# Strassen sets of a float32 MLP: weight blocks in fixed slots, low parts of the moving sums in reading order, and one weight sum made on VectorE instead of by an adding transfer

## The chip, the cores and the metric

The kernel runs on one core of a Trainium2 chip. Its metric is the device time of one execution in microseconds (us). The core has a matrix engine (TensorE, PE), VectorE (DVE), ScalarE (ACT), GpSimd (POOL) and SyncE (SP), which each take their instructions in order and meet at semaphores. SP and POOL start transfers here.

## The reference, cut to what matters

One layer of a streaming encoder in float32, for 512 prompt frames, 16 meta tokens and 64 sample frames. What the change touches is the MLP, on 576 tokens, with `D_MODEL` 1024 and `D_FF` 4096:

```python
h = _layer_norm(ALPHA * h + (mix @ w_out + b_out), ln1_g, ln1_b)
f = jnp.square(jax.nn.relu(h @ w_mlp1 + b_mlp1)) @ w_mlp2 + b_mlp2
h = _layer_norm(ALPHA * h + f, ln2_g, ln2_b)
```

## The kernel before

**Splitting.** A float32 product is made of three matmuls on a faster type: each operand is rounded to a high part (`hi`) and the difference to a low part (`lo`); hi x hi, hi x lo and lo x hi are added in PSUM. Of a weight block ACT makes the high part (`op_hi`, L1839) and DVE the low part (`op_lo`, L2695). Of a moving operand of the second MLP product it is ACT's `v_hi` (L1895) or `block_hi` (L1881) and DVE's `set_lo` (L2764).

**Sets.** The first 8 output blocks of the first MLP product are done plainly. All the rest but the last quarter of the second product is done in 12 sets (`SETS`), t = 0 to 11, each a 2 x 2 block product in Winograd's form with 7 instead of 8 block products: "out" (second product) for t = 0, 1, 4, 5, 8, 9 and "in" (first product) for t = 2, 3, 6, 7, 10, 11. The 7 steps of a set are s = 0 to 6. A step is 24 matmuls of 288 columns with 128 x 128 weights (`block_product`, L1268 to L1270).

**Weight blocks.** A set has 4 blocks of 128 x 1024 in DRAM (`wsets_d[t, 0..3]`, 512 KB each). The 7 stationary operands are, in the order of the steps: AL = block 0; SI = 2 + 3; X = 0 + 2 + 3; DE = 1; AP = 0 + 2; DP = 1 + X; GA = block 3. There are five slots: `raw` 0 to 3 and `w_fifth` (slot 4). `set_slots(t)` gives a (AL, then X), b (DE, then DP), c (SI), d (AP) and g (GA); a/c and b/d change places from set to set. SP loads block 2 into c and POOL adds block 3 with an adding transfer (L3203); SP loads block 2 into d and POOL adds block 0 (L3205). X and DP are made on DVE (`x_sum` L2681 in step 6 of the set before, `dp_sum` L2687 in step 2).

**Order around it.** Everything is written out by hand. High and low parts have three homes in turn; in step s of set t ACT makes the high and DVE the low part of the operand for step s + 2, and ACT may do so once step s - 1 is done. PE's step waits for its low part (`s_lo`), for its PSUM banks and for its moving operand. The banks: step 2 waits for `first_copied` (ACT, L1845), step 4 for `third_sum` (DVE, L2725; in an "out" set for its second `out_add`, L2713), step 6 for `fourth_sum` (DVE, L2733; or the fourth `out_add`).

**The moving sums.** An "in" set gives four blocks of relu-squared, C11, C22, C12, C21 (ACT: L1874 relu, L1881 high part, L1886 square in place). From them DVE makes V5, T3, V6, V4 (`v_sum`, L2744 to L2754). With B11, B22 and B21 (C11, C22, C21) they are the seven moving operands of the next "out" sets, read in the order B11, V5, V6, B21, T3, B22, V4. Much of this is done under the next set, as its tail (`set_tail` on ACT, `tail` and `sums` on DVE). An "out" set with group 0 (t = 4, 8) follows at once on the "in" set that makes its operands and waits for each in turn (`moving_ready`); C11 of a set is rounded in step 4, C22 in 5, C12 in 6, C21 in step 0 of the next. Sets with a tail under them are t = 3, 4, 7, 8 and 11. In sets 0 and 1 ACT and DVE have extra work: `residual2` (L1906), `hs_round`, `hs_low`.

Of the kernel before, what the change touches and what calls it, by code (L numbers as in the profile page):

```python
# [69 lines left out]

def set_slots(t):


    return (1, 3, 0, 2, 4) if t % 2 == 0 else (0, 2, 1, 3, 4)


def source_slot(t, s):
    a, b, c, d, g = set_slots(t)
    return (a, c, a, b, d, b, g)[s]
# [125 lines left out]
def encoder_step(nc, x, wstream, wsets_d, vecs_d, bv_d, kc_d, vc_d, state_d, wpool_d, y_out, k_out, v_out, s_out):  # L205
    with ExitStack() as ctx:
# [185 lines left out]
        al_in, de_in, ga_in, si_base = x_in[0]  # L392
        ap_base = x_in[1][0]
        si_in, ap_in = sem("si_in"), sem("ap_in")
        x_made, dp_made = sem("x_made"), sem("dp_made")
# [262 lines left out]
        def _(sp):  # L658
# [30 lines left out]
            sp.wait_ge(lo_split, U_MLP1 + HIDDEN - 3)  # L689
            load_block(0, set_slots(0)[2], 2, si_base)  # L690
            sp.wait_ge(lo_split, U_MLP1 + HIDDEN - 2)
            load_block(0, set_slots(0)[0], 0, al_in)
            sp.wait_ge(lo_split, U_MLP1 + HIDDEN - 1)
            load_block(0, set_slots(0)[3], 2, ap_base)
            sp.wait_ge(lo_split, U_MLP1 + HIDDEN)
            load_block(0, set_slots(0)[1], 1, de_in)
            sp.wait_ge(f_lo_done, F_TILES)
            load_block(0, set_slots(0)[4], 3, ga_in)
            for t in range(1, N_SETS):
                a, b, c, d, g = set_slots(t)  # L700
                o = OPS * (t - 1)
                sp.wait_ge(s_lo, o + W_SI + 1)
                sp.wait_ge(x_made, t)
                load_block(t, a, 0, al_in)
                sp.wait_ge(s_lo, o + W_X + 1)
                sp.wait_ge(dp_made, t)
                load_block(t, c, 2, si_base)
                sp.wait_ge(s_lo, o + W_AP + 1)
                load_block(t, b, 1, de_in)
                sp.wait_ge(s_lo, o + W_DP + 1)  # L710
                load_block(t, d, 2, ap_base)
                sp.wait_ge(s_lo, o + W_GA + 1)
                load_block(t, g, 3, ga_in)
# [637 lines left out]
        def _(act):  # L1351
# [472 lines left out]
            def op_hi(o):  # L1824
                t, s = divmod(o, OPS)
                if o >= OPS * N_SETS:
                    return
                landed = {W_AL: al_in, W_SI: si_in, W_DE: de_in, W_AP: ap_in, W_GA: ga_in}.get(s)
                if landed is not None:
                    act.wait_ge(landed, (0 if s in (W_SI, W_AP) else SET_IN) + 16 * (t + 1))  # L1830
                elif s == W_X:
                    act.wait_ge(x_made, t + 1)
                else:
                    act.wait_ge(dp_made, t + 1)
                if o < 3:
                    act.wait_ge(unit_done, U_MLP1 + HIDDEN - 2 + o)
                else:
                    act.wait_ge(op_done, o - 2)
                nc.scalar.activation(op_home(o)[0], set_home(source_slot(t, s)), ACT.Copy).then_inc(s_hi, 1)  # L1839

# [107 lines left out]
            def set_tail(t, s):  # L1948

                _, p, g = SETS[t]  # L1950
                if s == 0:
                    block_relu(t, C21)
                    if p == 3:
                        block_hi(t, C21)
                    block_plain(t, C21)
                elif p < 3:
                    v_hi(t, T3)
                    v_hi(t, V4)

            for t in range(N_SETS):  # L1960
# [3 lines left out]
                for s in range(OPS):  # L1964
                    if s == 0 and tail is not None:
                        set_tail(tail, 0)
                        op_hi(o + 2)
                        if SETS[tail][1] < 3:
                            v_hi(tail, V6)
                            v_hi(tail, B21)  # L1970
                        continue
# [10 lines left out]
                    if kind == "in" and s == 6:  # L1982
                        block_relu(t, C12)
                        if p == 3:
                            block_hi(t, C12)
                        block_plain(t, C12)
                    op_hi(o + s + 2)
                    if t == 0 and s == 0:
                        for f in (V6, T3, V4):
                            sum_hi(f, PRS - 1)  # L1990
                    if s == 1 and tail is not None:
                        set_tail(tail, 1)
                    if kind == "in" and s == 5:
                        block_relu(t, C22)
                        block_hi(t, C22)
                        block_plain(t, C22)
                    if kind == "in" and s == 6 and p < 3:
                        v_hi(t, V5)
                    if t == 0 and s < 4:
                        residual2((4, 0, 2, 6)[s])  # L2000
                        residual2((5, 1, 3, 7)[s])
                    if t == 1 and 1 <= s <= 4:
# [88 lines left out]
        def _(dve):  # L2091
# [583 lines left out]
            def x_sum(t):  # L2675

                if t == N_SETS:
                    return
                a, _, c, _, _ = set_slots(t)
                dve.wait_ge(si_in, 16 * (t + 1))  # L2680
                tt(set_home(a), set_home(c), set_home(a), ALU.add).then_inc(x_made, 1)  # L2681

            def dp_sum(t):

                a, b, _, _, _ = set_slots(t)
                dve.wait_ge(x_made, t + 1)
                tt(set_home(b), set_home(b), set_home(a), ALU.add).then_inc(dp_made, 1)  # L2687

            def op_lo(o):
# [133 lines left out]
            for t in range(N_SETS):  # L2823
# [162 lines left out]
        def _(pool):  # L2986
# [213 lines left out]
            for t in range(N_SETS):  # L3200
                _, _, c, d, _ = set_slots(t)
# [98 lines left out]
```

## Time and profile before

| | us |
|---|---|
| median of 3 runs | 799.43 |
| lowest, highest | 797.58, 800.34 |
| the profiled execution | 798.34 |
| its span | 796.6 |

The profile is of one execution. Its page gives the busy time of each engine; matmul rows overlap, so a busy PE isn't yet a PE without gaps, and the gaps are read in the timeline. A row of the timeline names in square brackets how long its engine sat idle before it and whose event ended that. A wait for several events is put down to the one that came last by the profile. L numbers are lines of the kernel before.

### The profile page before, as it was taken

To read this page: it belongs to the slowest core of one execution; us is meant where nothing else is said; L and a number is where in the kernel's file an instruction comes from. 1 tells how busy PE (TensorE), PEld (TensorE's weight loads), DVE (VectorE), ACT (ScalarE), POOL (GpSimd) and SP (SyncE) were. 2 spreads that over 40 slices of the span, in tenths; PEclk is the share of its full clock that TensorE was granted. 3 is DMA by queue.
4 is the path that set the end of the run, shared out by engine and by line. 5 is a ranking of instruction groups with operands and counts; after the bars stand their busy time and mean duration, and the time that the engine had idled before them with its cause. 6 is when DMAs were issued, how large, how long until landed. Compare 5 with 4: busy or idle time off the path is not lost.

```text
span 796.6 us, 14048 instructions
## 1 busy us (share of the span) xinstructions
PE 776.4 (97%) x5720; PEld 748.6 (94%) x5720; DVE 519.6 (65%) x762; ACT 426.8 (54%) x666; POOL 145.9 (18%) x195
## 2 busy tenths in 40 slices
PE   8999999999999999999999999999999999999995
PEld 7999899999989999999999999998999999999994
DVE  6823344754546476876968979687775887655644
ACT  5633345655646465563655556587336763477324
POOL 2100000472220110006640000000000000000356
PEclk9999999999999999999999999999999999999998
DMA  8632131112111112233112366645666456653203
GB/s 313 261 123 95 58 114 53 54 57 81 53 53 54 53 53 73 88 114 125 58 50 80 80 190 176 163 123 143 186 173 171 130 141 175 173 125 133 80 2 119
DMA packets 27070, 90.57 MB, mean 114 GB/s; under 512 B 2864, under 2 KB 7104, under 8 KB 26624
## 3 DMA queue, kind: packets, MB, share of 16 engines
q1 hardware_dynamic: 22592, 74.26, 27.3%
q0 software_dynamic: 4000, 15.10, 10.3%
q8 instruction: 45, 0.74, 0.4%
q10 hardware_dynamic: 416, 0.33, 0.1%
q14 instruction: 17, 0.14, 0.1%
HBM read 84.84 MB, written 4.85 MB: 113 GB/s over the span
## 4 chain that ended last, share of the span: by engine, by line
PE 80%; DVE 7%; ACT 6%; issue 3%; DMA 3%; DVEq 0%; ACTq 0%; POOL 0%; SPq 0%; POOLq 0%
PE lin L751 8%; PE lin L752 8%; PE lin L753 8%; PE z L1268 6%; PE z L1269 6%; PE z L1270 6%; PE z L1007 3%; DMA raw<-w_sets 3%; PE lin L1145 3%; PE lin L1146 3%; PE lin L1147 3%; PE lin L1285 2%; PE lin L1287 2%; PE lin L1286 2%; PE lin L1268 2%
## 5 line engine op out<-in xcount | busy, mean ns | idle before, releaser
L751 PE MATMUL lin<-h_hi,whi 128*128 128x288 f32 (+1 forms) x448 | 133.8, 299 | 0.0
L752 PE MATMUL lin<-h_lo,whi 128*128 128x288 f32 (+1 forms) x448 | 132.5, 296 | 0.0
L753 PE MATMUL lin<-h_hi,wlo 128*128 128x288 f32 (+1 forms) x448 | 132.0, 295 | 0.0
L751 PEld LDWEIGHTS lin<-h_hi,whi 128*128 128x128 f32 x448 | 84.2, 188 | 1.3 <-issue 1.1
L752 PEld LDWEIGHTS lin<-h_lo,whi 128*128 128x128 f32 x448 | 84.2, 188 | 0.1
L753 PEld LDWEIGHTS lin<-h_hi,wlo 128*128 128x128 f32 x448 | 84.3, 188 | 0.0
L1839 ACT ACTIVATE whi<-raw 128x1024 fp32r<-128x1024 f32 x48 | 50.7, 1056 | 55.4 <-DMA raw<-w_sets 18.0
L2695 DVE TENSOR_TENSOR wlo<-raw,whi 128x1024 fp32r<-128x1024 f32 x48 | 58.7, 1223 | 22.3 <-ACT whi L1839 22.3
L2098 DVE TENSOR_TENSOR wlo<-raw,whi 128x1024 fp32r<-128x1024 f32 x41 | 50.9, 1242 | 28.6 <-ACT whi L1361 26.5
L1361 ACT ACTIVATE whi<-raw 128x1024 fp32r<-128x1024 f32 x38 | 40.0, 1053 | 50.5 <-PE lin L753 32.5
L1268 PE MATMUL z<-f_ops,whi 128*128 128x288 f32 x176 | 52.8, 300 | 3.4 <-DVE f_ops L2764 2.0
L1269 PE MATMUL z<-f_ops,whi 128*128 128x288 f32 x176 | 52.3, 297 | 0.0
L1270 PE MATMUL z<-f_ops,wlo 128*128 128x288 f32 x176 | 52.2, 296 | 0.0
L3203 POOL DMA_DIRECT2D raw<-w_sets x12 | 10.5, 872 | 191.9 <-DMA raw<-w_sets 191.9
L1839 ACT ACTIVATE third_hi<-raw 128x1024 fp32r<-128x1024 f32 x24 | 25.3, 1056 | 25.8 <-DVE raw L2681 7.3
L1268 PEld LDWEIGHTS z<-f_ops,whi 128*128 128x128 f32 x176 | 33.8, 192 | 3.8 <-issue 2.2
L2695 DVE TENSOR_TENSOR third_lo<-raw,third_hi 128x1024 fp32r<-128x1024 f32 x24 | 29.3, 1222 | 11.3 <-ACT third_hi L1839 11.3
L2319 DVE SCALAR_TENSOR_TENSOR sa<-z,sa 128x512 f32<-128x512 f32 (+4 forms) x25 | 19.8, 795 | 25.6 <-ACT sa L1544 25.4
L1270 PEld LDWEIGHTS z<-f_ops,wlo 128*128 128x128 f32 x176 | 33.7, 192 | 0.0
L1269 PEld LDWEIGHTS z<-f_ops,whi 128*128 128x128 f32 x176 | 33.7, 191 | 0.0
L2282 DVE TENSOR_SCALAR gates<-lin,vecs 128x288 f32<-128x288 f32 x16 | 8.2, 516 | 34.6 <-PE lin L753 34.6
L1268 PE MATMUL z<-hs_hi,whi 128*128 128x288 f32 x96 | 28.6, 298 | 0.9 <-DVE z L2725 0.6
(456 smaller groups left out, 2572.7 us busy)
## 6 DMA issues: line engine op xcount, KB each, us to landing
raw<-w_stream SPq DMA_DIRECT2D x64, 512.0 KB, 3.2
raw<-w_sets SPq DMA_DIRECT2D x48, 512.0 KB, 3.6
raw<-w_sets POOLq DMA_DIRECT2D x24, 512.0 KB, 6.9
w_fifth<-w_sets SPq DMA_DIRECT2D x12, 512.0 KB, 6.2
r<-x_t SPq DMA_DIRECT2D x8, 296.0 KB, 4.4
kcache<-k_cache SPq DMA_DIRECT2D x1, 2048.0 KB, 9.8
vcache<-v_cache SPq DMA_DIRECT2D x1, 2048.0 KB, 8.0
y<-r SPq DMA_DIRECT2D x8, 160.0 KB, 1.8
```

The source lines that it names most:

```text
L751: pe.matmul(out, w_h, hi, start=first, stop=False)
L752: pe.matmul(out, w_h, lo, start=False, stop=False)
L753: return pe.matmul(out, w_l, hi, start=False, stop=last)
L1007: last = pe.matmul(zf[:, d:d + w], stationary[:, :], part[:, src + at:src + at + w], start=False, stop=True, skip_group_check=True)
L1145: pe.matmul(out, w_h, hi, start=first, stop=False)
L1268: pe.matmul(out, w_h, hi, start=s < 2 and i == 0, stop=False, skip_group_check=True)
L1269: pe.matmul(out, w_h, lo, start=False, stop=False, skip_group_check=True)
L1270: last = pe.matmul(out, w_l, hi, start=False, stop=i == PRS - 1, skip_group_check=True)
L1361: nc.scalar.activation(whi[:, j % SPLIT, :], raw[:, j, :], ACT.Copy).then_inc(hi_split, 1)
L1839: nc.scalar.activation(op_home(o)[0], set_home(source_slot(t, s)), ACT.Copy).then_inc(s_hi, 1)
L2098: tt(wlo[:, j % SPLIT, :], raw[:, j, :], whi[:, j % SPLIT, :].bitcast(F32), ALU.subtract)\
L2695: tt(home[1], set_home(source_slot(t, s)), home[0].bitcast(F32), ALU.subtract).then_inc(s_lo, 1)
```

## The change

The slots are the same for every set: a = 1, b = 3, c = 0, d = 2, g = 4. AP is no longer loaded and added to: DVE makes it as X - GA (`ap_sum`, in step 1). For set 0 GA's block is loaded into d as well, ahead of the rest, and subtracted there. The second adding transfer of a set goes, and so does the load of its base (in set 0 it becomes that load of block 3).

SP now loads c first, once `x_sum` is made, then a, once `dp_sum` is made, then b and g. `dp_sum` goes from step 2 to step 3, ahead of `op_lo`.

The low part of B11 goes behind `op_lo` of step 5, that of V5 from step 0 of the next set to step 6, ahead of `x_sum`. V4's sum goes behind `op_lo` of step 0. B21 stays in step 1, T3 goes from 1 to 2, B22 from 2 to 4 and V4 from 3 to 4. On ACT the rounding of V5 goes ahead of `op_hi` of step 6, that of B21 from step 0 to 1, that of V4 from 1 to 3, and the `residual2` of set 0 from steps 0 to 3 to steps 1, 2, 4, 5.

```diff
-def set_slots(t):
-    return (1, 3, 0, 2, 4) if t % 2 == 0 else (0, 2, 1, 3, 4)
+def set_slots():
+    return 1, 3, 0, 2, 4
@@ sync: loads of the sets
-            load_block(0, set_slots(0)[3], 2, ap_base)
+            load_block(0, set_slots()[3], 3, ga_first)
...
                 sp.wait_ge(s_lo, o + W_SI + 1)
                 sp.wait_ge(x_made, t)
+                load_block(t, c, 2, si_base)
+                sp.wait_ge(dp_made, t)
                 load_block(t, a, 0, al_in)
-                sp.wait_ge(s_lo, o + W_X + 1)
-                sp.wait_ge(dp_made, t)
-                load_block(t, c, 2, si_base)
-                sp.wait_ge(s_lo, o + W_AP + 1)
+                sp.wait_ge(s_lo, o + W_DP + 1)
                 load_block(t, b, 1, de_in)
-                sp.wait_ge(s_lo, o + W_DP + 1)
-                load_block(t, d, 2, ap_base)
                 sp.wait_ge(s_lo, o + W_GA + 1)
                 load_block(t, g, 3, ga_in)
@@ scalar: op_hi
-                elif s == W_X:
-                    act.wait_ge(x_made, t + 1)
+                elif s in (W_X, W_AP):
+                    act.wait_ge(x_made if s == W_X else ap_made, t + 1)
@@ scalar: set_tail and the loop of the sets
-                    v_hi(t, T3)
-                    v_hi(t, V4)
+                    for o in {1: (B21, T3), 3: (V4,)}.get(s, ()):
+                        v_hi(t, o)
...
                             v_hi(tail, V6)
-                            v_hi(tail, B21)
...
                         block_plain(t, C12)
+                        if p < 3:
+                            v_hi(t, V5)
                     op_hi(o + s + 2)
...
-                    if s == 1 and tail is not None:
-                        set_tail(tail, 1)
+                    if s and tail is not None:
+                        set_tail(tail, s)
...
-                    if kind == "in" and s == 6 and p < 3:
-                        v_hi(t, V5)
-                    if t == 0 and s < 4:
-                        residual2((4, 0, 2, 6)[s])
-                        residual2((5, 1, 3, 7)[s])
+                    if t == 0 and s in (1, 2, 4, 5):
+                        m = {1: 4, 2: 0, 4: 2, 5: 6}[s]
+                        residual2(m)
+                        residual2(m + 1)
@@ vector
+            def ap_sum(t):
+                a, _, _, d, g = set_slots()
+                if t == 0:
+                    g = d
+                    dve.wait_ge(ga_first, SET_IN + 16)
+                else:
+                    dve.wait_ge(ga_in, SET_IN + 16 * (t + 1))
+                dve.wait_ge(x_made, t + 1)
+                tt(set_home(d), set_home(a), set_home(g), ALU.subtract).then_inc(ap_made, 1)
...
-                        if sums:
-                            set_lo(tail, V5)
-                            v_sum(tail, V4)
                     if inner:
                         if s == 3:
                             third_sum(t)
                         elif s == 5:
                             fourth_sum(t)
-                            last_lo(t, C11) if p == 3 else set_lo(t, B11)
+                        elif s == 6 and p < 3:
+                            v_sum(t, V5)
+                            v_sum(t, T3)
                     elif s >= 2:
                         out_add(t, s - 2)
-                    if s == 6 and inner and p < 3:
-                        v_sum(t, V5)
-                        v_sum(t, T3)
-                    if s == 2:
+                    if s == 3:
                         dp_sum(t)
+                    elif s == 1:
+                        ap_sum(t)
                     op_lo(o + s + 2)
...
                     if sums:
-                        for f in {0: (V6,), 1: (B21, T3), 2: (B22,), 3: (V4,)}.get(s, ()):
+                        if s == 0:
+                            v_sum(tail, V4)
+                        for f in {0: (V6,), 1: (B21,), 2: (T3,), 4: (B22, V4)}.get(s, ()):
                             set_lo(tail, f)
...
+                    if inner and s == 5:
+                        last_lo(t, C11) if p == 3 else set_lo(t, B11)
...
                             v_sum(t, V6)
+                            set_lo(t, V5)
                     if s == 6:
                         x_sum(t + 1)
@@ gpsimd
                 pool.dma_start(set_home(c), wsets_d[t, 3], accum_op=ALU.add).then_inc(si_in, 16)
-                pool.wait_ge(ap_base, SET_IN + 16 * (t + 1))
-                pool.dma_start(set_home(d), wsets_d[t, 0], accum_op=ALU.add).then_inc(ap_in, 16)
```

## Rows read from the trace of the kernel before

**Rows 1.** The page: the span, and busy us of PE and DVE.

```profile
span 796.6 us, 14048 instructions
...
PE 776.4 (97%) x5720; PEld 748.6 (94%) x5720; DVE 519.6 (65%) x762; ACT 426.8 (54%) x666; POOL 145.9 (18%) x195
```

**Rows 2.** Windows of sets 6, 7, 8 and 9: length, then busy us.

```profile
core 0: us, PE busy (x) PEld busy (x) DVE busy (x) ACT busy (x) POOL busy (x), PEclk, DMA share, GB/s
593.95:616.28 22.33, 22.33 (x170) 22.33 (x169) 13.09 (x14) 13.69 (x20) 1.73 (x2) 1.00 0.72 173
616.28:639.93 23.65, 22.80 (x170) 22.40 (x169) 20.01 (x24) 18.16 (x29) 1.73 (x2) 1.00 0.51 147
639.93:663.83 23.90, 22.53 (x171) 22.13 (x169) 19.37 (x23) 11.79 (x17) 0.92 (x3) 1.00 0.60 153
663.83:685.86 22.03, 22.03 (x171) 22.03 (x169) 15.44 (x16) 8.81 (x9) 2.55 (x3) 1.00 0.66 170
```

**Rows 3.** Timeline of PE, first matmuls of steps: start us, us, ..., [idle before].

```profile
461.88 0.37 PE L1268 MATMUL z<-f_ops,whi 128*128 128x288 f32 x1 [1.43 <-DVE wlo L2695]
...
550.99 0.37 PE L1268 MATMUL z<-f_ops,whi 128*128 128x288 f32 x1 [1.99 <-DVE f_ops L2764]
...
623.09 0.37 PE L1268 MATMUL lin<-hs_hi,third_hi 128*128 128x288 f32 x1 [0.26 <-ACT z L1845]
...
630.28 0.37 PE L1268 MATMUL lin<-hs_hi,whi 128*128 128x288 f32 x1 [0.59 <-DVE z L2725]
...
636.74 0.30 PE L1268 MATMUL lin<-hs_hi,whi 128*128 128x288 f32 x1
...
644.41 0.37 PE L1268 MATMUL z<-f_ops,third_hi 128*128 128x288 f32 x1 [1.14 <-DVE f_ops L2764]
```

**Rows 4.** Window behind the wait at 550.99; the number before the last two is PEclk.

```profile
551.65:555.05 3.40, 3.40 (x16) 3.40 (x15) 2.76 (x3) 3.40 (x6) 0.00 (x0) 0.50 0.36 135
```

**Rows 5.** Groups by line on DVE: busy us, mean ns of one.

```profile
L2695 DVE TENSOR_TENSOR wlo<-raw,whi 128x1024 fp32r<-128x1024 f32 x48 | 58.7, 1223 | 22.3 <-ACT whi L1839 22.3
...
L2681 DVE TENSOR_TENSOR raw<-raw 128x1024 f32<-128x1024 f32 x12 | 14.6, 1219 | 0.0
...
L2764 DVE TENSOR_TENSOR f_ops<-f_plain,f_ops 128x576 fp32r<-128x576 f32 x24 | 17.7, 752 | 0.0
```

**Rows 6.** Timeline of DVE in sets 6 to 8.

```profile
615.80 0.76 DVE L2744 TENSOR_TENSOR f_plain<-f_b,f_b 128x576 f32<-128x576 f32 x1 [2.02 <-ACT f_b L1886]
...
618.95 1.22 DVE L2681 TENSOR_TENSOR raw<-raw 128x1024 f32<-128x1024 f32 x1
...
629.38 0.76 DVE L2725 TENSOR_TENSOR z<-lin,f_plain 128x576 f32<-128x576 f32 x1
...
642.38 1.22 DVE L2681 TENSOR_TENSOR raw<-raw 128x1024 f32<-128x1024 f32 x1
643.51 0.75 DVE L2764 TENSOR_TENSOR f_ops<-f_plain,f_ops 128x576 fp32r<-128x576 f32 x1
```

**Rows 7.** Timeline of ACT in set 0 and in sets 7 and 8.

```profile
461.15 0.63 ACT L1845 ACTIVATE lin<-z 128x576 f32<-128x576 f32 x1
...
616.62 0.67 ACT L1895 ACTIVATE f_ops<-f_plain 128x576 fp32r<-128x576 f32 x1
...
629.73 0.90 ACT L1874 ACTIVATE f_b<-z,vecs 128x288 f32<-128x288 f32 x2 [0.98 <-PE z L1270]
...
631.83 1.04 ACT L1839 ACTIVATE whi<-w_fifth 128x1024 fp32r<-128x1024 f32 x1
...
639.47 1.06 ACT L1839 ACTIVATE third_hi<-raw 128x1024 fp32r<-128x1024 f32 x1 [0.89 <-DMA raw<-w_sets]
```

**Rows 8.** The adding transfer for SI, L3203, from issue to landing.

```profile
DMA to landing us min/median/max: 5.4/7.7/9.1
```

**Rows 9.** The loads of the sets by SP, L687, from issue to landing.

```profile
DMA to landing us min/median/max: 3.1/4.0/8.8
```

More of the change, by code:

```diff
@@ L68, in sets_before, with source_slot @@
     return sum(k == kind for k, _, _ in SETS[:t])
-def set_slots(t):
-    return (1, 3, 0, 2, 4) if t % 2 == 0 else (0, 2, 1, 3, 4)
-def source_slot(t, s):
-    a, b, c, d, g = set_slots(t)
+def set_slots():
+    return 1, 3, 0, 2, 4
+def source_slot(s):
+    a, b, c, d, g = set_slots()
     return (a, c, a, b, d, b, g)[s]
@@ L392, in encoder_step @@
         al_in, de_in, ga_in, si_base = x_in[0]
-        ap_base = x_in[1][0]
-        si_in, ap_in = sem("si_in"), sem("ap_in")
+        ga_first = x_in[1][0]
+        si_in, ap_made = sem("si_in"), sem("ap_made")
         x_made, dp_made = sem("x_made"), sem("dp_made")
@@ L689, in _ @@
             sp.wait_ge(lo_split, U_MLP1 + HIDDEN - 3)
-            load_block(0, set_slots(0)[2], 2, si_base)
+            load_block(0, set_slots()[2], 2, si_base)
             sp.wait_ge(lo_split, U_MLP1 + HIDDEN - 2)
-            load_block(0, set_slots(0)[0], 0, al_in)
+            load_block(0, set_slots()[0], 0, al_in)
             sp.wait_ge(lo_split, U_MLP1 + HIDDEN - 1)
-            load_block(0, set_slots(0)[3], 2, ap_base)
+            load_block(0, set_slots()[3], 3, ga_first)
             sp.wait_ge(lo_split, U_MLP1 + HIDDEN)
-            load_block(0, set_slots(0)[1], 1, de_in)
+            load_block(0, set_slots()[1], 1, de_in)
             sp.wait_ge(f_lo_done, F_TILES)
-            load_block(0, set_slots(0)[4], 3, ga_in)
+            load_block(0, set_slots()[4], 3, ga_in)
             for t in range(1, N_SETS):
-                a, b, c, d, g = set_slots(t)
+                a, b, c, d, g = set_slots()
                 o = OPS * (t - 1)
@@ L1827, in op_hi @@
                     return
-                landed = {W_AL: al_in, W_SI: si_in, W_DE: de_in, W_AP: ap_in, W_GA: ga_in}.get(s)
+                landed = {W_AL: al_in, W_SI: si_in, W_DE: de_in, W_GA: ga_in}.get(s)
                 if landed is not None:
-                    act.wait_ge(landed, (0 if s in (W_SI, W_AP) else SET_IN) + 16 * (t + 1))
-                elif s == W_X:
-                    act.wait_ge(x_made, t + 1)
+                    act.wait_ge(landed, (0 if s == W_SI else SET_IN) + 16 * (t + 1))
+                elif s in (W_X, W_AP):
+                    act.wait_ge(x_made if s == W_X else ap_made, t + 1)
                 else:
@@ L1838, in op_hi @@
                     act.wait_ge(op_done, o - 2)
-                nc.scalar.activation(op_home(o)[0], set_home(source_slot(t, s)), ACT.Copy).then_inc(s_hi, 1)
+                nc.scalar.activation(op_home(o)[0], set_home(source_slot(s)), ACT.Copy).then_inc(s_hi, 1)
             def first_copy(t):
@@ L2678, in x_sum @@
                     return
-                a, _, c, _, _ = set_slots(t)
+                a, _, c, _, _ = set_slots()
                 dve.wait_ge(si_in, 16 * (t + 1))
                 tt(set_home(a), set_home(c), set_home(a), ALU.add).then_inc(x_made, 1)
+            def ap_sum(t):
[7 more added lines that the diff above has]
+                tt(set_home(d), set_home(a), set_home(g), ALU.subtract).then_inc(ap_made, 1)
             def dp_sum(t):
-                a, b, _, _, _ = set_slots(t)
+                a, b, _, _, _ = set_slots()
                 dve.wait_ge(x_made, t + 1)
@@ L2694, in op_lo @@
                 dve.wait_ge(s_hi, o + 1)
-                tt(home[1], set_home(source_slot(t, s)), home[0].bitcast(F32), ALU.subtract).then_inc(s_lo, 1)
+                tt(home[1], set_home(source_slot(s)), home[0].bitcast(F32), ALU.subtract).then_inc(s_lo, 1)
             def out_add(t, n):
@@ L3200, in _ @@
             for t in range(N_SETS):
-                _, _, c, d, _ = set_slots(t)
+                _, _, c, d, _ = set_slots()
                 pool.wait_ge(si_base, SET_IN + 16 * (t + 1))
                 pool.dma_start(set_home(c), wsets_d[t, 3], accum_op=ALU.add).then_inc(si_in, 16)
-                pool.wait_ge(ap_base, SET_IN + 16 * (t + 1))
-                pool.dma_start(set_home(d), wsets_d[t, 0], accum_op=ALU.add).then_inc(ap_in, 16)
             pool.wait_ge(n2_d0, 2)
```

## The prediction

> **What bounds the kernel now.** I read first the page, for busy shares. TensorE (PE) is busy 776.4 of 796.6 us and VectorE (DVE) 519.6 [rows 1], so what can be won is what PE waits, and what can be lost is anything that makes PE wait more. Then the sets one by one, as windows [rows 2]. Set 9 takes 22.03 us, 3.15 a step, and is the pace of an "out" set without a wait; set 6 takes 22.33, 3.19 a step, the pace of an "in" set. Set 7 takes 23.65 and set 8 23.90. There DVE is busy 20.01 of 23.65 us, against 13.09 in set 6 and 15.44 in set 9. So the moving sums that are finished under the next set load DVE to 85% just where PE waits. Sets 3 and 4 are built the same way. I call 3 and 4, and 7 and 8, a crossing.
>
> Then the timeline of PE, for the waits themselves [rows 3]. Set 7 waits at step 2 (0.26 us shown, step start 623.09 where 616.28 + 2 x 3.19 = 622.66 was due) and at step 4 (0.59, for `third_sum`). Set 8 waits at step 1 (1.14, for V5's low part), set 4 at the same place (1.99), set 0 at step 2 (1.43). Behind the 1.99 the clock was granted at 0.50 for 3.4 us [rows 4]: 1.2 instead of 2.4 GHz. By the windows sets 7 and 8 are 1.3 and 1.9 us over their paces; sets 3 and 4 lose 2.0 more (0.85 of wait, the rest clock), set 0 some 1.6: 10 us in all, and more than that can't be won in the sets.
>
> Last the timelines of DVE and ScalarE (ACT) in the crossing [rows 5, 6, 7]. I write times from the start of set 7, R = 616.28, and hi(n), lo(n) for the rounding on ACT and the difference on DVE of the block for step n (n = 7 and 8 belong to the next set). A long DVE operation lasts 1.22 us, a short one 0.75 [rows 5]; with the next in the queue they follow at 1.14 and 0.67 (642.38 to 643.51 is one long step [rows 6]). A hand-over between ACT and DVE is 0.03 to 0.05, one from PE 0.2.
>
> **Part 1, the transfers.** Gone are the load and the adding transfer for the AP block, 12 adding transfers and 11 loads of 512 KB. No wait of PE ends on a transfer, so they are worth nothing by themselves. What a transfer does hold is ACT: hi(8) in set 7 began at 639.47 after 0.89 us of waiting for one [rows 7], the adding transfer for SI, which takes 5.4 to 9.1 us [rows 8]. Its base is now loaded right behind `x_sum`, some three steps sooner, so that wait goes. But the rounding of V5 now stands ahead of hi(8) on ACT and waits for V5's sum on DVE. Step 6 began at 636.74 [rows 3]; 0.2 for the hand-over, 1.6 for C12's three operations, 0.76 for V5's sum, 0.67 for its rounding [rows 6, 7], and hi(8) comes at about 640.0. Worth: nothing.
>
> The other side: the AL load now waits for `dp_made` in step 3 (before: `x_sum` in step 0), and is wanted by hi(7) in step 5, 4.4 us later. Loads from SP land in 3.1 to 8.8 us, median 4.0 [rows 9]: 0 to 4.4 us late, and I take 0 by the median. A gain is excluded, since the load comes later than before.
>
> **Part 2, the subtraction.** `ap_sum` is as long as `x_sum`, 1.22 us [rows 5], 12 times, 14.6 us of DVE. Between crossings DVE has 6 to 9 us of a set free [rows 2], and the block is due a step later than it is made: nothing. In a crossing it is 1.14 us in a full queue.
>
> **Part 3, the order.** Two edits build round trips that were not there. (a) V5: sum on DVE, rounding on ACT, then hi(8) on ACT, lo(8) on DVE, V6's sum, V5's low part, and only then `x_sum`. (b) `dp_sum` stands right ahead of lo(5) in step 3, and hi(5) needs it: DVE 1.22, ACT 1.05, DVE 1.22 in line, with DVE idle in the middle, and in "in" sets ACT's work on C11 behind it. Without a tail of sums (b) fits: from the start of step 3, 0.95 + 1.2 + 1.05 + 1.25 = 4.45 us, and step 5 is due at 6.3. So sets 2, 5, 6, 9, 10, 11 cost nothing. In set 1 the four `hs_low`, twice the columns of a short operation and so by estimate from [rows 5] 1.4 us each, bring `out_add` 3 to about 0.5 us past step 6: +0.5.
>
> The crossing, worked through in queue order. V5 sum ends at 0.3 (615.80 [rows 6]), its rounding at 1.0 (616.62 was its start before, too [rows 7]), hi(1) at 1.95, lo(1) at 3.2; step 1 starts 3.35. V6's sum 3.9, V5 low 4.55, `x_sum` 5.7 (before: 618.95 + 1.22, so 3.9 [rows 6]). hi(2) 6.8, lo(2) 8.05: **step 2 starts 8.2**, before 6.8 (623.09 [rows 3]). V4's sum and V6 low 9.4, `ap_sum` 10.5, lo(3) 11.65, B21 low 12.3, lo(4) 13.5, T3 low 14.1, `third_sum` 14.8, `dp_sum` 15.95. hi(5) 17.05, lo(5) 18.3; step 5 starts 18.45. ACT: V4's rounding 17.6, C11 19.7 (its four operations took from 629.73 to 631.83 [rows 7]), hi(6) 20.6. lo(6) 21.9, then B22 and V4 low, which are now in step 4, 23.2, `fourth_sum` 23.85. Step 6 waits for that: **it starts 24.0**, before 20.46 (636.74 [rows 3]). Set 7 ends at 27.2 instead of 23.65: +3.5.
>
> Set 8, from its own start. C22 and C12 on ACT follow `fourth_sum` and end 0.45; V5 sum 1.25, rounding 1.95, hi(1) 2.9, lo(1) 4.2, V6 sum 4.85, V5 low 5.5: **step 1 at 5.65**, before 4.48 (644.41 [rows 3]). `x_sum` 6.65, hi(2) 7.75, lo(2) 9.0, V4's sum, V6 low 10.35: **step 2 at 10.5**, since an "out" set reads V6 there. `ap_sum`, lo(3), B21 low, `out_add` 0, lo(4), T3 low, `out_add` 1, `dp_sum` end 17.6; hi(5), lo(5) 19.95, `out_add` 2 20.6, lo(6) 21.8, B22 low 22.45: **step 5 at 22.6**, since it reads B22. Then two steps of 3.15: 28.9 instead of 23.90 [rows 2]: +5.0.
>
> Sets 3 and 4 have the same order. Before they lost 2.0 us more, 0.85 at V5's low part (1.99 against 1.14 [rows 3]) and the rest on the clock; the new schedule replaces both, so it is +6.5 for this pair where it is +8.5 for 7 and 8.
>
> Set 0: step 2 began 461.88 [rows 3]. Its wait is put down to DVE, but a step 2 needs `first_copied` as well, and that copy ran 461.15 to 461.78 [rows 7], behind two `residual2`. These move behind hi(3): about -0.7.
>
> **The clock.** Of the waits in the sets of before only the one of 1.99 us is followed by a fall [rows 3, 4]; at 3.15 us for 24 matmuls 26 fit into its 3.40 us, and 16 were in it; that is 1.3 lost, and by half the clock 1.7 at most: I take 1.4. The new schedule has waits of 1.6 to 2.7 us, five in each crossing. A fall ahead of a longer wait costs nothing; behind step 5 of set 4 or 8 it costs 1.4. I count one of these two: +1.4.
> The Trainium skill, TensorE: Matmul & The Clock Gate, in its section on a second failure mode, says that TensorE idling briefly but often between groups of matmuls swings between the two clocks. The trace agrees once in several waits; by that rule every wait would bring a fall, and the sum would be the heavy case below.
>
> **Sum** against the profiled execution, 798.3 us: -0.7 + 0.5 + 6.5 + 8.5 + 1.4 = +16.2, so 814.5; the median of the runs is 1.1 higher: 815.6, said as 815.5. A measurement of this kernel tells about 0.3%, 2.4 us, from no change.
>
> **Rivals.** *Faster: the late transfer was the cause.* The chain of waits of set 8's step 1 leads through the adding transfer. If the sooner SI base and V5's low part ahead of `x_sum` make that step punctual, sets 4 and 8 get back 2.2 + 1.4 and 1.3 (waits with their hand-over), the waits for `third_sum` 0.8 twice, set 0 0.7: 7.2, so 792.2. It decides at V5's low part, which must end by 3.0 in set 8, that is 642.9. Against it: even with set 7 as it was hi(8) comes at 640.0 (above), and lo(8), V6's sum and V5's low part end at 643.6 (before: 643.51 + 0.75 [rows 6]). Chance 0.07.
> The Trainium skill, DMA: Bandwidth & Descriptors, section on issuing engines, says that the queues of all engines run on the same 16 DMA engines and interleave; by this every removed transfer speeds the rest, which would help this rival. No row here prices it.
> *No change*: what V5 wins, `x_sum` loses, and (b) is absorbed: 799.4, chance 0.05. For it: each edit alone is about 1 us. Against: DVE is at 85% in the crossing, with little to absorb it.
> *Half of it*: only step 2 of sets 3 and 7 (1.4 each) and B22 at step 5 of sets 4 and 8 (0.85 each, the least by the length of lo(5), `out_add`, lo(6) and B22 low after step 3) get later: +4.5, so 804. Chance 0.08.
> *Heavy*: falls of the clock also after step 2 of sets 3 and 7 (0.7 net each) and after both steps 5, or the AL load 1 us late at each crossing: 818 to 825. Chance 0.10, half of it over 822.
> The forecast keeps 0.70.
>
> **Range.** 805 to 822: the forecast with 10 below for a queue that recovers between steps, and up into the heavy case. Left out are "faster" 0.07, "no change" 0.05, half of "half of it" 0.04 and half of "heavy" 0.05: 0.21. Faster 0.07, same 0.05, slower 0.88.
>
> **What would show it.** In the changed profile: windows of sets 3 and 7 near 27 us, of 4 and 8 near 28 to 29, the others at 22.0 to 22.4; PE waiting in set 7 at step 2 for lo(2), at step 6 for `fourth_sum`, in set 8 at step 5 for a sum's low part; DVE idle about 1 us ahead of lo(5), released by ACT; nothing at all waiting for SI. It is wrong if `third_sum` of set 7 ends before 13.9 after the set's start, or if set 7's step 6 starts before 21.

## The result and the profile after

| | us |
|---|---|
| median before (4 runs) | 798.96 |
| median changed (4 runs, 815.59 to 817.89) | 816.62 |
| ratio | 1.0222, 95% interval 1.0198 to 1.0246 |
| span of the profiled execution | 796.6 before, 815.3 changed |

The changed kernel is 17.7 us slower; 815.5 was forecast. The two profiled executions differ by 18.7 us in span. Of these the 12 sets, 276.8 us before and 294.9 after, hold 18.0; another 0.5 had gone before the first set began. In the tables a set's length runs from its first matmul to that of the next (for set 11 to the end of its last matmul), and "step n" is the time from the set's start to the first matmul of step n, read from PE's timeline.

| set | before | forecast | changed |
|---|---|---|---|
| 0 | 23.69 | 23.0 | 23.18 |
| 1 | 22.03 | 22.5 | 22.75 |
| 3 | 23.66 | 27.2 | 27.28 |
| 4 | 26.02 | 28.9 | 30.38 |
| 7 | 23.65 | 27.2 | 28.67 |
| 8 | 23.89 | 28.9 | 28.95 |
| the other six | 133.9 | as before | 133.7 |

The windows of sets 6, 7, 8 and 9 of the changed kernel, which answer to [rows 2] (length, busy us of PE, PEld, DVE, ACT and POOL, then PEclk, DMA share, GB/s):

```profile
602.40:624.73 22.33, 22.33 (x170) 22.33 (x169) 13.34 (x14) 13.18 (x19) 0.86 (x1) 1.00 0.43 119
624.73:653.40 28.67, 24.91 (x170) 23.89 (x169) 21.00 (x25) 18.44 (x29) 0.87 (x1) 0.94 0.34 93
653.40:682.36 28.96, 24.43 (x171) 23.82 (x169) 22.62 (x26) 12.96 (x17) 0.87 (x1) 0.94 0.34 91
682.36:704.39 22.03, 22.03 (x171) 22.03 (x169) 16.25 (x17) 7.97 (x8) 0.87 (x1) 1.00 0.44 120
```

DVE's work in set 7 rose by 1.0 us and the set by 5.0. So it isn't the added work that fills the time. The DMA share fell from 0.51 to 0.34, and no time was won by it.

Where PE waits now, by its timeline (start, us, ..., [idle before <-releaser]; L numbers are lines of the kernel whose trace is shown). These rows answer to [rows 3]:

```profile
461.43 0.40 PE L1265 MATMUL z<-f_ops,whi 128*128 128x288 f32 x1 [0.50 <-DVE wlo L2704]
...
555.56 0.37 PE L1265 MATMUL z<-f_ops,whi 128*128 128x288 f32 x1 [2.25 <-DVE f_ops L2773]
...
572.40 0.37 PE L1265 MATMUL z<-f_ops,third_hi 128*128 128x288 f32 x1 [2.35 <-DVE f_ops L2773]
...
632.82 0.40 PE L1265 MATMUL lin<-hs_hi,third_hi 128*128 128x288 f32 x1 [1.37 <-DVE third_lo L2704]
...
648.74 0.58 PE L1265 MATMUL lin<-hs_hi,whi 128*128 128x288 f32 x1 [2.24 <-DVE f_plain L2742]
...
657.58 0.37 PE L1265 MATMUL z<-f_ops,third_hi 128*128 128x288 f32 x1 [0.84 <-DVE f_ops L2773]
...
662.41 0.37 PE L1265 MATMUL z<-f_ops,whi 128*128 128x288 f32 x1 [1.39 <-DVE f_ops L2773]
...
674.44 0.37 PE L1265 MATMUL z<-f_ops,whi 128*128 128x288 f32 x1 [2.30 <-DVE f_ops L2773]
```

In set 7 PE waits at step 2 for lo(2) (L2704), and at step 6 for `fourth_sum` (L2742). In set 8 it waits at steps 1, 2 and 5, each time for the low part of a sum (L2773). The working of the forecast has all of them. The sign that it gave for being wrong did not come either: `third_sum` of set 7 (the row at 638.76 below) ends 14.8 us after the set's start, as worked out, and not before 13.9.

Why they are late stands in DVE's timeline of set 7, which answers to [rows 6] (times from the set's start are these less 624.73):

```profile
624.25 0.76 DVE L2753 TENSOR_TENSOR f_plain<-f_b,f_b 128x576 f32<-128x576 f32 x1 [2.02 <-ACT f_b L1883]
...
626.71 1.23 DVE L2704 TENSOR_TENSOR wlo<-raw,whi 128x1024 fp32r<-128x1024 f32 x1 [1.03 <-ACT whi L1836]
...
629.19 1.22 DVE L2678 TENSOR_TENSOR raw<-raw 128x1024 f32<-128x1024 f32 x1
631.53 1.23 DVE L2704 TENSOR_TENSOR third_lo<-raw,third_hi 128x1024 fp32r<-128x1024 f32 x1 [1.13 <-ACT third_hi L1836]
...
638.76 0.76 DVE L2734 TENSOR_TENSOR z<-lin,f_plain 128x576 f32<-128x576 f32 x1
639.43 1.22 DVE L2696 TENSOR_TENSOR raw<-raw 128x1024 f32<-128x1024 f32 x1
641.77 1.23 DVE L2704 TENSOR_TENSOR third_lo<-raw,third_hi 128x1024 fp32r<-128x1024 f32 x1 [1.13 <-ACT third_hi L1836]
645.36 1.23 DVE L2704 TENSOR_TENSOR wlo<-w_fifth,whi 128x1024 fp32r<-128x1024 f32 x1 [2.37 <-ACT whi L1836]
646.51 1.42 DVE L2773 TENSOR_TENSOR f_ops<-f_plain,f_ops 128x576 fp32r<-128x576 f32 x2
647.84 0.75 DVE L2742 TENSOR_TENSOR f_plain<-lin,f_plain 128x576 f32<-128x576 f32 x1
```

In set 7 the engine with the longest queue stands idle five times, 7.7 us in all, and each time for ACT; before it was three times, 3.6 us. The wait of 2.02 for C12's blocks at the end of the set is the same in both kernels. The other four make 5.7 us, where the kernel before had 1.6: 1.03 after V5's and T3's sums, 1.13 after `x_sum` (L2678), 1.13 after `dp_sum` (L2696) and 2.37 until ACT has done C11. Then two lows (646.51) still stand ahead of `fourth_sum`, on which PE waits.

The adding transfers did what they were said to. On the page of the changed kernel the adding transfers land sooner (7.7 us median for SI before [rows 8]) and are 12 instead of 24:

```profile
raw<-w_sets SPq DMA_DIRECT2D x37, 512.0 KB, 3.3
raw<-w_sets POOLq DMA_DIRECT2D x12, 512.0 KB, 5.4
```

ACT waited for an adding transfer 8 times before, 24.6 us in all, and now once, 1.4 us, in set 0. But in the crossings it now waits for the AL load ahead of hi(7), 0.72 us in set 4 and 1.76 in set 8:

```profile
673.85 1.06 ACT L1836 ACTIVATE third_hi<-raw 128x1024 fp32r<-128x1024 f32 x1 [1.76 <-DMA raw<-w_sets]
```

DVE has other work until 675.54 and PE doesn't wait for this low part, so the lateness costs nothing.

### The profile page after: what moved, and what is told of

The parts are those of the page before. It is cut to its first block, busy times and chain, and to the rows that moved or that the text cites. A ratio compares the mean times of both kernels' runs of the same rounds, so it can differ in the third digit from the quotient of the medians.

```text
span 815.3 us, 14037 instructions
## 1 busy us (share of the span) xinstructions
PE 784.0 (96%) x5719; PEld 754.0 (92%) x5720; DVE 533.3 (65%) x774; ACT 427.0 (52%) x666; POOL 135.6 (17%) x183
## 4 chain that ended last, share of the span: by engine, by line
PE 72%; DVE 13%; ACT 9%; issue 5%; DVEq 0%; ACTq 0%; POOL 0%; POOLq 0%
PE lin L748 8%; PE lin L749 7%; PE lin L750 7%; PE z L1265 4%; PE z L1266 4%; PE z L1267 4%; PE z L1004 3%; DVE wlo L2704 3%; PE lin L1142 3%; PE lin L1143 2%; PE lin L1144 2%; PE lin L1282 2%; PE lin L1284 2%; PE lin L1283 2%; ACT whi L1836 2%
## 5 line engine op out<-in xcount | busy, mean ns | idle before, releaser
L2704 DVE TENSOR_TENSOR wlo<-raw,whi 128x1024 fp32r<-128x1024 f32 x48 | 58.7, 1222 | 26.9 <-ACT whi L1836 26.9
L1265 PE MATMUL z<-f_ops,whi 128*128 128x288 f32 x176 | 53.8, 306 | 6.4 <-DVE f_ops L2773 5.9
L3215 POOL DMA_DIRECT2D raw<-w_sets x12 | 10.5, 872 | 287.7 <-DMA raw<-w_sets 287.7
L1266 PE MATMUL z<-f_ops,whi 128*128 128x288 f32 x176 | 53.0, 301 | 0.0
L2704 DVE TENSOR_TENSOR third_lo<-raw,third_hi 128x1024 fp32r<-128x1024 f32 x24 | 29.4, 1223 | 17.2 <-ACT third_hi L1836 17.2
```

The costliest lines, as they stand in the source:

```text
L1265: pe.matmul(out, w_h, hi, start=s < 2 and i == 0, stop=False, skip_group_check=True)
L1266: pe.matmul(out, w_h, lo, start=False, stop=False, skip_group_check=True)
L2704: tt(home[1], set_home(source_slot(s)), home[0].bitcast(F32), ALU.subtract).then_inc(s_lo, 1)
```

## The experiments

The theory: the order on DVE and ACT costs the time, by V5's place, by that of `dp_sum` and by the late lows of B22 and V4; the subtraction and the transfers cost nearly nothing. The rivals: the 14.6 us that the subtraction adds to DVE, and the later loads. Each ratio is against runs of the kernel before beside it; times are medians of 4 to 10 runs.

**E1, the slots, loads and subtraction alone.** From the changed kernel, the order of the kernel before put back on both engines:

```diff
+                        if sums:
+                            set_lo(tail, V5)
+                            v_sum(tail, V4)
...
-                    if s == 3:
+                    if s == 2:
                         dp_sum(t)
...
-                        for f in {0: (V6,), 1: (B21,), 2: (T3,), 4: (B22, V4)}.get(s, ()):
+                        for f in {0: (V6,), 1: (B21, T3), 2: (B22,), 3: (V4,)}.get(s, ()):
...
-                            set_lo(t, V5)
```

> Fixed slots, the loads and the subtraction of the changed kernel, but every operation of ScalarE and VectorE in the order of the kernel before (dp_sum in step 2, V5's rounding behind hi(8), its low part in step 0 behind x_sum, B22 low in step 2, V4 low in step 3, residual2 in steps 0 to 3). Theory (the two round trips and the late low parts cost the time, the subtraction nothing): sets 3 and 7 0.45 us longer through ap_sum ahead of third_sum, set 8 0.2 shorter and set 4 2.3 shorter because the SI block no longer comes late, so about 797.5 us. Rival VectorE (the 12 x 1.22 = 14.6 us of the subtraction are what went into the time): about 813 us. Rival transfers (later loads from SP): about 815 us, with ScalarE waiting for transfers.

Measured: 797.49 us, ratio 0.9995 (0.9981 to 1.0008). Sets 3 and 7 take 24.05 and 24.03 (0.4 more), sets 4 and 8 23.69 and 23.65 (2.3 and 0.2 less), all as expected. In the profiled executions the sets are 2.1 us shorter in total; in the runs nothing of that is to be seen (797.49 against 797.43). The before of the profile had a fall of the clock in set 4, at a mean granted clock of 0.994. One such fall (3.4 us at half clock) is 0.002 of a run's mean clock, by my estimate, and of the 13 runs of before beside E1 all but the slowest lie at 0.995 to 0.997, as do the ten of E1. So most of these runs probably had no such fall and less to win; that is read from rounded means and isn't shown by a trace.

```profile
614.47:638.51 24.04, 22.81 (x171) 22.40 (x170) 21.19 (x26) 19.05 (x30) 0.86 (x1) 1.00 0.40 111
638.51:662.16 23.65, 22.53 (x171) 22.13 (x169) 22.09 (x26) 11.78 (x16) 0.86 (x1) 1.00 0.43 112
```

With the subtraction DVE is busy 22.09 of 23.65 us in set 8, and the set is no longer than before. The rivals of 813 and 815 us are out.

**E2, the order alone**, on the kernel before with its slots and all its transfers; both engines in the changed order.

> The kernel before with its slots, its transfers and its two adding transfers a set, no subtraction, but with the order of the changed kernel on ScalarE and VectorE, dp_sum in step 3 included. Theory (order): the crossing keeps both round trips and loses only ap_sum's 1.14 us from the queue, about 1.0 us less in sets 3 and 7 and 1.1 less in sets 4 and 8 than in the changed kernel: about 812.5 us, four falls of the clock as there. Rival VectorE (subtraction): about 802 us. Rival transfers (later loads from SP): about 799 us.

Measured: 815.17 us, ratio 1.0234 (1.0208 to 1.0259). The rivals of 802 and 799 us are out, and the order without the subtraction costs as much as the whole change. The sum is made up otherwise than expected, though. The four sets of the crossings take 110.0 us for 115.3 in the changed kernel, with two falls of the clock instead of four. Sets 1, 5, 6 and 9 take 3.8 us more, which the theory's 812.5 did not have. In sets 3 and 5 ACT waits for the old adding transfer, 1.34 and 7.91 us, and their step 1 begins late; in set 3 at 4.73 instead of 3.28:

```profile
526.34 1.06 ACT L1839 ACTIVATE whi<-raw 128x1024 fp32r<-128x1024 f32 x1 [1.34 <-DMA raw<-w_sets]
...
528.71 0.41 PE L1268 MATMUL z<-hs_hi,whi 128*128 128x288 f32 x1 [1.39 <-DVE wlo L2695]
```

So with the new order the old transfers are late now and then, and with the old order the new ones change nothing that the runs show.

**E3 to E6 and E8, parts undone one at a time** in the changed kernel.

E3, V5's rounding, its low part and V4's sum in their old places:

```diff
                         block_plain(t, C12)
-                        if p < 3:
-                            v_hi(t, V5)
                     op_hi(o + s + 2)
...
+                    if kind == "in" and s == 6 and p < 3:
+                        v_hi(t, V5)
...
+                        if sums:
+                            set_lo(tail, V5)
+                            v_sum(tail, V4)
...
-                            set_lo(t, V5)
```

> The changed kernel with one part undone: V5 is rounded behind hi(8) on ScalarE, its low part and V4's sum stand at the start of step 0 of the next set, behind x_sum and ahead of lo(2). dp_sum stays in step 3, B22 and V4 low in step 4. Theory: worked through in queue order, step 2 of sets 3 and 7 begins 6.5 us after the set's start instead of 8.1, step 6 at 22.2 instead of 24.0, step 5 of sets 4 and 8 at 20.2 instead of 22.4: 4.2 us less in each crossing, about 808 us. If V5's place is the whole cause (rival): 800 us. If it is none of it: 816 us.

E4, `dp_sum` in step 2:

```diff
-                    if s == 3:
+                    if s == 2:
                         dp_sum(t)
```

> The changed kernel with one part undone: dp_sum in step 2, ahead of lo(4), as before; the rest as changed, V5's rounding ahead of hi(8) and B22 and V4 low in step 4 included. Theory: ScalarE reaches hi(6) about 2.3 us sooner, step 6 of sets 3 and 7 begins at 22.5 instead of 24.0, but step 4 1.1 us late for third_sum; set 8's step 5 at 20.5 instead of 22.4: 3.6 us less in each crossing, about 809 us. If dp_sum's place is the whole cause (rival): 800 us. If it is none of it: 816 us.

E5, the lows of T3, B22 and V4 in their old steps, and V4's rounding in step 1:

```diff
-                    for o in {1: (B21, T3), 3: (V4,)}.get(s, ()):
+                    for o in {1: (B21, T3, V4)}.get(s, ()):
...
-                        for f in {0: (V6,), 1: (B21,), 2: (T3,), 4: (B22, V4)}.get(s, ()):
+                        for f in {0: (V6,), 1: (B21, T3), 2: (B22,), 3: (V4,)}.get(s, ()):
```

> The changed kernel with one part undone: T3 low in step 1, B22 low in step 2, V4 low in step 3 and V4's rounding in step 1, as before; both round trips stay. Theory: step 6 of sets 3 and 7 begins at 22.9 instead of 24.0, and step 5 of sets 4 and 8 is punctual, but third_sum comes later: 2.9 us less in each crossing, about 811 us. If the late low parts are the cause (rival): 800 us.

E6, E3 and E4 together:

> The changed kernel with both round trips undone: V5's rounding, its low part and V4's sum as before, and dp_sum in step 2; B22 and V4 low stay in step 4. Theory: in queue order step 6 of sets 3 and 7 is punctual, set 7 takes 23.3 us, set 8 24.9; with set 0's gain about 797 us, within 2 us of the kernel before. If the late low parts of B22 and V4 are a third cause by themselves (rival): above 802 us.

E8, of E3 only the rounding on ACT; V5's low part stays ahead of `x_sum`:

> The changed kernel with half of the V5 part undone: V5 is rounded behind hi(8) again, but its low part stays ahead of x_sum in step 6 and V4's sum behind lo(2). It tells the round trip through ScalarE from the longer queue ahead of x_sum. Theory: step 2 of sets 3 and 7 begins at 7.05 instead of 8.1, step 6 at 22.95, step 5 of sets 4 and 8 at 21.6: 2.1 us less in each crossing, about 812 us, against 805 where x_sum's place is put back as well. If the round trip alone is what V5's move costs (rival): 805 us.

Measured, with step starts of set 7 and 8 from PE's timeline:

| | us | ratio, interval | 7: step 2 | 7: step 6 | set 7 | 8: step 5 | set 8 | falls in the sets |
|---|---|---|---|---|---|---|---|---|
| before | | 1 | 6.81 | 20.46 | 23.65 | 17.60 | 23.89 | 1 |
| changed | 816.62 | 1.0222 | 8.09 | 24.01 | 28.67 | 21.03 | 28.95 | 4 |
| E3 | 804.98 | 1.0098 (1.0081, 1.0115) | 6.41 | 21.66 | 26.45 | 18.56 | 24.93 | 2 |
| E4 | 806.88 | 1.0119 (1.0102, 1.0136) | 8.09 | 22.51 | 25.71 | 20.50 | 26.91 | 0 |
| E5 | 808.18 | 1.0125 (1.0103, 1.0147) | 8.09 | 22.77 | 26.04 | 20.53 | 26.98 | 1 |
| E6 | 798.79 | 1.0004 (0.9989, 1.0019) | 6.41 | 20.18 | 23.37 | 18.40 | 24.82 | 1 |
| E8 | 811.58 | 1.0162 (1.0140, 1.0184) | 6.96 | 22.88 | 27.67 | 19.78 | 27.69 | 4 |

By the ratios, E3 gives back 1.2 points of 2.2, E4 1.0, E5 1.0, and E3 and E4 together (E6) all of it. No single part is the cause, and the one-cause rivals (800 us, in E8 805) and "none of it" (816) are out. E3's and E4's gains add up to that of E6 (2.3 for 2.2). The third part doesn't add: undone alone the late lows are worth 1.0 point, but E6 still has them and is as fast as before. Against E1, which has none of the three (nor the small moves of B21, B11 and `residual2`), it is 0.1 point slower; in the profiles its sets 3 and 7 are 0.7 us shorter each, set 8 is 1.2 longer and set 4, which has a fall of the clock in E6, 2.4. So the late lows cost that much only where the two round trips have used up the room in the queue.

E8 against E3 parts V5's move: with the rounding alone put back step 2 begins at 6.96, which is 1.13 us sooner; `x_sum` behind V5's low part costs the other 0.6.

The expected step starts of set 7 held within 0.15 us (6.5, 22.5, 22.9, 7.05, 22.95); E3's step 6 came 0.5 sooner. In set 8 E4's step 5 held (20.5), while those of E3 and E8 came 1.6 to 1.8 sooner than expected (20.2 and 21.6), counted from a set start that a fall of the clock had made late. The times of E3, E4 and E5 are 2 to 3 us under the expected ones. Part of that is the kernel before, which beside E3 and E4 ran 1.5 us and beside E5 0.5 us faster than beside the changed kernel; the falls of the clock that each of them loses, and the expectations left in, are another part. How the rest divides isn't shown.

The windows of sets 7 and 8 of E6. DVE has as much to do in the two together as in E1 (43.1 us for 43.3). Set 7 is 0.3 us shorter than before, set 8 0.9 longer (expected 23.3 and 24.9):

```profile
617.24:640.61 23.37, 22.69 (x170) 22.39 (x169) 19.81 (x24) 17.84 (x29) 0.86 (x1) 1.00 0.38 114
640.61:665.43 24.82, 22.83 (x170) 22.26 (x169) 23.29 (x27) 13.05 (x17) 0.87 (x1) 1.00 0.38 106
```

**E9, the price of the subtraction by itself**, on E1:

```diff
+                if t:
+                    tt(set_home(d), set_home(a), set_home(g), ALU.subtract).then_inc(ap_once, 1)
+                    dve.wait_ge(ap_once, t)
                 tt(set_home(d), set_home(a), set_home(g), ALU.subtract).then_inc(ap_made, 1)
```

> The kernel of e1 (order of the kernel before, slots and subtraction of the changed one) with the subtraction made twice in sets 1 to 11, the second after a wait for the first, so some 1.25 us of VectorE more in a set. It prices the subtraction by itself. Theory: it is hidden in every set but those with a tail; there it stands ahead of third_sum or the second out_add, and step 4 of sets 3, 4, 7 and 8 begins 1.2 us later (15.6, 15.35): 4 x 1.2 = 4.9 us, about 802.4 us. Rival (VectorE's load counts wherever it is): 11 x 1.25 = 13.8 us, 811 us. Rival (hidden everywhere): 797.5 us.

Measured: 803.36 us, ratio 1.0062 (1.0038 to 1.0085), near the theory's 802.4 and far from 811 and 797.5. Step 4 of sets 3, 7 and 8 begins at 15.69, 15.66 and 15.40, as expected; sets 1, 2, 5, 6, 9 and 10 are within 0.25 of E1. Set 11, which has the last blocks under it, is 1.0 longer, which was not expected. In the window of set 7 DVE has 1.2 us more and the set is 1.27 longer; in set 9 it has 1.2 more and the set is the same:

```profile
617.82:643.12 25.30, 23.07 (x170) 22.42 (x169) 22.38 (x27) 19.14 (x30) 0.87 (x1) 1.00 0.37 105
643.12:668.02 24.90, 22.78 (x170) 22.17 (x169) 23.30 (x27) 11.90 (x16) 0.87 (x1) 1.00 0.37 106
668.02:690.05 22.03, 22.03 (x170) 22.03 (x169) 17.48 (x18) 7.98 (x8) 0.87 (x1) 1.00 0.43 120
```

**E7, an order made from the same working.** Slots, loads and subtraction of the changed kernel. In words: V5 is rounded behind hi(8). Between two "in" sets `x_sum` comes right behind lo(8), then V6's sum, lo(2), V5 low, V4's sum; all other lows come in step 3 or later. Ahead of an "out" set V6's sum and V5 low stand ahead of `x_sum`, V4's sum and V6 low ahead of lo(2) (V6's rounding ahead of hi(2)), B22 low in step 3, V4 low in step 5. `dp_sum` is in step 2, but in step 3 in set 0 and in "out" sets with a tail. A sum's low part is written over the sum, so V4's sum must stand ahead of V6 low and B21 low, and T3's ahead of B22 low. The core:

```diff
+                    to_out, to_in = sums and not inner, sums and inner
+                    if s == (3 if to_out or t == 0 else 2):
                         dp_sum(t)
-                    elif s == 1:
+                    elif s == 1 and not sums:
                         ap_sum(t)
+                    if to_out:
+                        if s == 0:
+                            v_sum(tail, V4)
+                        for f in {0: (V6,), 2: (T3,), 3: (B22,), 5: (V4,)}.get(s, ()):
+                            set_lo(tail, f)
+                    elif to_in and s == 1:
+                        v_sum(tail, V4)
                     op_lo(o + s + 2)
...
+                    if (to_out and s == 0) or (to_in and s == 3):
+                        v_sum(tail, T3)
+                    if to_out and s == 1:
+                        set_lo(tail, B21)
+                    if to_in:
+                        for f in {0: (V5,), 3: (V6, B21, B22), 5: (T3, V4)}.get(s, ()):
+                            set_lo(tail, f)
+                    if sums and s == 1:
+                        ap_sum(t)
```

> A schedule of its own on the changed kernel's slots, loads and subtraction. V5 is rounded behind hi(8). Between two in sets x_sum stands right behind lo(8), and all lows but V5's wait until step 3 or later; ahead of an out set V6's sum and V5 low stand ahead of x_sum, V4's sum and V6 low ahead of lo(2), B22 low in step 3. dp_sum is in step 2 but for set 0 and the out sets with a tail. Theory (what bounds the crossing is the order of the queues of VectorE and ScalarE, and hardly their load): in queue order sets 3 and 7 take 22.3 us without a wait, sets 4 and 8 23.3, set 0 23.0, no fall of the clock: 7 us less in the sets than before, about 791 us. Rival (VectorE is simply full there, 20 to 21 us of work in a set of 22): no order helps, 797 us or more.

Measured: 793.20 us, ratio 0.9934 (0.9917 to 0.9950), so 0.7% faster than the kernel before and 2.2 us slower than expected; "797 or more", the rival of a full VectorE, is out. Sets 3 and 7 take 22.33 and 22.32, sets 4 and 8 23.42 and 23.41, set 0 23.03, and the clock doesn't fall in the sets:

```profile
612.95:635.27 22.32, 22.32 (x171) 22.32 (x169) 20.57 (x24) 18.25 (x29) 0.87 (x1) 1.00 0.40 119
635.27:658.68 23.41, 23.09 (x171) 22.35 (x169) 22.75 (x27) 12.67 (x17) 0.87 (x1) 1.00 0.38 113
```

In set 7 PE has no wait left, with DVE at 92%. In set 8 DVE is at 97% and idle for 0.7 us in all. Of the rival "simply full" the 1.4 us that set 8 still takes over the pace of 22.03 may be left; no run takes work from DVE there, so that isn't shown.

**E10, `dp_sum` in step 3 in the order of E7:**

```diff
-                    if s == (3 if to_out or t == 0 else 2):
+                    if s == 3:
                         dp_sum(t)
```

> The kernel of e7 with dp_sum in step 3 in every set. It asks whether dp_sum's place costs by itself. Theory (it costs only where it comes late behind other lateness): in the schedule of e7 third_sum ends by 10.6 and dp_sum by 11.8, hi(5) by 12.8, before C11 can begin at 13.0, so sets 3 and 7 stay at 22.3; only set 1 with its four hs_low gets 0.65 longer: about 793.8 us. Rival (the round trip costs by itself what e4 gave back, some 4 us in a crossing): about 801 us.

Measured: 797.07 us, ratio 0.9987 (0.9974 to 1.0000): 4 us more than E7, and half way between the two expectations (793.8 and 801). Set 7 takes 23.19. DVE's timeline from step 2 of set 7:

```profile
621.91 1.22 DVE L2696 TENSOR_TENSOR raw<-raw,w_fifth 128x1024 f32<-128x1024 f32 x1
624.25 1.23 DVE L2710 TENSOR_TENSOR wlo<-raw,whi 128x1024 fp32r<-128x1024 f32 x1 [1.12 <-ACT whi L1836]
625.39 0.76 DVE L2740 TENSOR_TENSOR z<-lin,f_plain 128x576 f32<-128x576 f32 x1
626.06 1.22 DVE L2702 TENSOR_TENSOR raw<-raw 128x1024 f32<-128x1024 f32 x1
628.40 1.23 DVE L2710 TENSOR_TENSOR third_lo<-raw,third_hi 128x1024 fp32r<-128x1024 f32 x1 [1.13 <-ACT third_hi L1836]
```

and of E7:

```profile
620.52 1.22 DVE L2696 TENSOR_TENSOR raw<-raw,w_fifth 128x1024 f32<-128x1024 f32 x1
621.66 1.22 DVE L2702 TENSOR_TENSOR raw<-raw 128x1024 f32<-128x1024 f32 x1
622.87 1.23 DVE L2710 TENSOR_TENSOR wlo<-raw,whi 128x1024 fp32r<-128x1024 f32 x1
```

My expectation overlooked that the subtraction has a round trip of its own: hi(4) needs `ap_sum` (L2696), and lo(4) needs hi(4). In E7 `dp_sum` (L2702) fills that time. Moved away it leaves two holes of 1.12 and 1.13 us where there was none. C11 on ACT then begins at 628.28, 1.0 us behind the end of step 3, and that lateness travels into set 8.

## Why the forecast held, point by point

**What bounds the kernel.** That the loss would lie in the crossings, but for small changes in sets 0 and 1, held: the other six sets changed by 0.2 us in all.

**Part 1, the transfers**, said to be worth nothing: E1, with the subtraction, shows it. SI's wait went; V5's rounding took its place. SP's loads now land in 3.3 us (median). The AL load, 0 to 4.4 us late by the bounds and taken at 0, was late by 0.72 us for ACT in set 4 and 1.76 in set 8, and cost nothing: 0 was right for the time, not for the transfer. The Trainium skill, DMA: Bandwidth & Descriptors, says in its section on issuing engines that transfers run on the same 16 DMA engines and interleave, whichever engine started them. The trace agrees in that SI's adding transfer lands in 5.4 us instead of 7.7 beside fewer others; its place in time was moved as well, so the gain isn't parted. No wait of PE hung on it.

**Part 2, the subtraction**, said to be hidden outside the crossings: E9 shows it for sets 1, 2, 5, 6, 9 and 10. In set 11 a second one was not hidden.

**Part 3, the order.** The working was right to 0.2 us up to the falls of the clock: step 2 of set 7 at 8.09 (8.2), step 5 at 18.32 (18.45), step 6 at 24.01 (24.0); in set 4 step 1 at 5.58 (5.65), step 2 at 10.40 (10.5), step 5 at 22.43 (22.6). Set 3 took 27.28 (27.2). What it did not say is how the parts share the loss: the two round trips about half each (E3, E4), and the late lows nearly nothing of their own (E6 against E1), though undone alone they look like half as well (E5). A small slip: sets 3 and 4 lost 2.1 us more than sets 7 and 8 before, not 2.0.

**Sets 0 and 1.** -0.5 for -0.7, +0.7 for +0.5. Set 0's step 2 came 0.9 us sooner once two `residual2` were out of the way of `first_copied`, though the wait was put down to DVE: the step begins at 6.95 to 6.97 in every kernel with the moved `residual2` and at 7.87 or 7.88 in E1, E9 and the kernel before, which have them in their old place. The set gave 0.4 of that back. `ap_sum` can be at most 0.2 of it, since E2, which has none, takes 22.98; the rest isn't explained.

**The clock** is the term that was mis-sized. One fall of two behind step 5 of sets 4 and 8 was counted, at 1.4 us; both came, and steps 5 of both sets last 4.78 us instead of 3.15, so 1.6 each: 3.3 us for 1.4. The count of one was a guess between none and two, and that both came is 1.9 of the 2.5 us that the profiled execution (817.1) lies over the sum's 814.5. The window behind the second:

```profile
675.75:679.15 3.40, 3.40 (x16) 3.40 (x16) 1.01 (x1) 0.00 (x0) 0.00 (x0) 0.50 0.25 94
```

The two other falls cost nothing, as said of falls ahead of a longer wait: the one from 648.45 made set 7 1.5 us longer, and set 8's step 1 then began at 4.18 instead of 5.58, since DVE had to finish anyway.

**The rivals.** "Late transfer" fell with its own condition: V5's low part ended 4.04 us after set 8's start, not by 3.0, and that start was 1.5 us late through the clock. "Half of it" and "no change" assumed a queue that catches up; the rows show it doing the opposite, since each hole on DVE is made by what ACT got late. The heavy case came in part, both steps 5, and stayed inside the range.

## What to carry to other kernels

When one in-order engine is the only one with little room, count its idle time ahead of each wait for another engine rather than its busy share: in set 7 it was idle for 7.7 us, and with the same work in the order of E7 for 1.8. An operation whose result goes through another engine and back needs other work placed behind it; filled with the next such operation the hole costs nothing, and an order that is sorted by when results are read doesn't see it. And delays in one chain need not add up: two of them did here, and the third, which seemed worth as much when undone alone, was worth almost nothing with the others gone. Undo them together before adding them up.

## What was not expected of the hardware

Of the changed kernel's waits of PE of 2.2 us and more, five in number, four had a stretch of 3.4 us at 1.2 GHz that began within 1.4 us behind them or in their last 0.3 us (set 3's step 6 had not); of the waits of 0.8 to 1.4 us none had one of its own. The kernel before has one such fall in its sets, at 551.7, behind a wait of 2.0. E1, E4, E7, E9 and E10, whose longest waits in the sets are shorter, show no fall in the sets at all; E2, E3, E5 and E6 show one or two, and E8 four. In the sets of all twelve kernels no wait of up to 1.7 us had a fall, while of the longer ones some had: in E6 a wait of 1.80 us had one and one of 1.78 had not, in E5 one of 2.24 had and one of 2.25 had not. So the length of a wait doesn't settle it alone. The Trainium skill, TensorE: Matmul & The Clock Gate, describes brief idling in its section on a second failure mode as a cause of swings between the clocks; it doesn't say that every wait brings one, as the prediction took it. The traces agree for the longer of these waits and not for the shorter ones.

The hand-over from DVE to ACT and back is nearly constant: in the changed kernel DVE was idle 1.12 or 1.13 us behind each of the 12 `dp_sum` and behind `x_sum` in sets 3, 4, 7 and 8, until ACT had rounded the 128 x 1024 block.
